# Forgetting attention and RG-LRU trunk on one core: the opening's matmuls in another order, and the forget sum inside the first key tile

## The reference, cut to what matters

```python
proj = x @ w_in
q, k, v, fg = jnp.split(proj, [D_MODEL, 2 * D_MODEL, 3 * D_MODEL], axis=-1)
...
log_f = jax.nn.log_sigmoid((fg + b_f).astype(jnp.float32))
c = jnp.cumsum(log_f, axis=1).transpose(0, 2, 1)
...
logits = jnp.einsum("bhqd,bhkd->bhqk", q_i, k).astype(jnp.float32) * scale
logits = logits + c_i[..., None] - c[:, :, None, :]
...
probs = jax.nn.softmax(logits, axis=-1)
```

## Time and profile before

| | us |
|---|---|
| median of 3 runs | 1261.48 (1260.67 to 1262.12) |
| the profiled execution | 1261.65 |
| its span in the trace | 1259.9 |
| TensorE busy | 1252.0 |
| GpSimd busy | 861.3 |
| VectorE busy | 537.0 |
| ScalarE busy | 408.9 |

### The profile page before, as it was taken

One profiled execution on the slowest core, in us unless ns is written; L12 is line 12 of the kernel. 1 busy time (PEld: TensorE's weight loads), 2 busy tenths in 40 slices (PEclk: granted clock), 3 DMA queues, 4 the chain that ended last, 5 costly groups with the idle time before them and its releaser, 6 DMA issues.

```text
span 1259.9 us, 17776 instructions
## 1 busy us (share of the span) xinstructions
PE 1252.0 (99%) x5893; PEld 1021.6 (81%) x5893; DVE 537.0 (43%) x832; ACT 408.9 (32%) x683; POOL 861.3 (68%) x1155
## 2 busy tenths in 40 slices
PE   9999999999999999999999999999999999999998
PEld 5777778788888888888888778888888888888887
DVE  6545545465344444201343375274444443301352
ACT  4445444224333434100144384014343433200041
POOL 7544557819877877777577646929877788777573
PEclk9999999999999999999999999999999999999999
DMA  5222132303322233333243222312222224333221
GB/s 196 69 67 67 52 115 89 112 17 109 108 88 95 100 122 111 110 92 100 67 167 103 81 84 84 117 51 100 100 100 100 91 93 133 118 100 94 74 92 59
DMA packets 57294, 120.63 MB, mean 96 GB/s; under 512 B 3761, under 2 KB 36081, under 8 KB 56737
## 3 DMA queue, kind: packets, MB, share of 16 engines
q1 hardware_dynamic: 56192, 117.45, 28.3%
q10 hardware_dynamic: 1056, 2.58, 0.6%
HBM read 117.83 MB, written 2.20 MB: 95 GB/s over the span
## 4 chain that ended last, share of the span: by engine, by line
PE 97%; DMA 1%; DVE 1%; ACT 1%; DVEq 0%; issue 0%; ACTq 0%; SPq 0%
PE bank L437 19%; PE bank L439 19%; PE bank L438 19%; PE bank L456 8%; PE bank L457 8%; PE bank L458 8%; PE bank L731 2%; PE bank L738 2%; PE bank L733 2%; PE bank L564 1%; PE bank L551 1%; PE bank L465 1%; PE bank L521 1%; PE bank L523 1%; DMA x<-xT 1%; PE bank L907 1%
## 5 line engine op out<-in xcount | busy, mean ns | idle before, releaser
L423 POOL TENSOR_TENSOR w_lo<-stage,w_hi 128x256 fp32r<-128x256 f32 x800 | 593.7, 773 | 29.5 <-issue 1.5
L417 POOL TENSOR_SCALAR w_hi<-stage 128x1024 fp32r<-128x1024 f32 x200 | 213.4, 1067 | 175.3 <-PE bank L458 77.3
L437 PE MATMUL bank<-x_hi,w_hi 128*128 128x512 f32 (+1 forms) x712 | 275.6, 387 | 0.0
L439 PE MATMUL bank<-x_hi,w_lo 128*128 128x512 f32 (+1 forms) x712 | 275.3, 387 | 0.0
L438 PE MATMUL bank<-x_lo,w_hi 128*128 128x512 f32 (+1 forms) x712 | 275.3, 387 | 0.0
L438 PEld LDWEIGHTS bank<-x_lo,w_hi 128*128 128x128 f32 x712 | 133.7, 188 | 27.3
L437 PEld LDWEIGHTS bank<-x_hi,w_hi 128*128 128x128 f32 x712 | 133.7, 188 | 27.1
L439 PEld LDWEIGHTS bank<-x_hi,w_lo 128*128 128x128 f32 x712 | 133.7, 188 | 26.9
L1150 DVE SCALAR_TENSOR_TENSOR tmp<-bank,cols,tmp 128x511 f32<-128x511 f32 x88 | 66.0, 750 | 201.3 <-ACT tmp L1431 190.3
L415 POOL TENSOR_TENSOR waiter<-waiter 128x1 f32<-128x1 f32 x101 | 21.1, 209 | 171.3 <-PE bank L439 119.0
L456 PE MATMUL bank<-w_hi,h_hi 128*128 128x512 f32 x352 | 137.3, 390 | 0.0
(11 more groups left out here) (182 smaller groups left out, 1806.5 us busy)
## 6 DMA issues: line engine op xcount, KB each, us to landing
stage<-w_square SPq DMA_DIRECT2D x163, 512.0 KB, 3.2
stage<-w_down SPq DMA_DIRECT2D x44, 512.0 KB, 3.6
rows<-norm_rows SPq DMA_DIRECT2D x4, 1024.0 KB, 6.2
outT<-x SPq DMA_DIRECT2D x7, 256.0 KB, 2.0
x<-xT SPq DMA_DIRECT2D x3, 512.0 KB, 6.9
p_in<-pT ACTq DMA_DIRECT2D x2, 512.0 KB, 3.4
w_ai<-w_lru SPq DMA_DIRECT2D x1, 1024.0 KB, 9.4
stage<-w_square ACTq DMA_DIRECT2D x1, 512.0 KB, 7.2
```

The source lines that it names most:

```text
L417: whole = pool.tensor_scalar(high[:, s, :], stage[:, s, :], 1.0, 0.0, ALU.mult, ALU.add)
L423: piece = pool.tensor_tensor(low[:, s, to], stage[:, s, to], high[:, s, to].bitcast(F32), ALU.subtract)
L437: pe.matmul(out, w_hi[:, s, c:c + P], m_hi, start=first, stop=False)
L439: return pe.matmul(out, w_lo[:, s, c:c + P], m_hi, start=False, stop=last)
```

## The change

On TensorE the first two blocks are turned ahead of the first forget products, as soon as the first pair of x is there. The high pass of the first query tile is cut in two: k = 0 to 3 stand behind blocks 2 and 3, and so ahead of the forget products of x tiles 4 to 7; k = 4 to 7 stand behind block 4. `sum_forget` moves from behind the key tile into it, behind step k = 5. On VectorE `c_rows` is made ahead of `queries(0)`. On ScalarE the store of `c_rows` stands ahead of the key tile's copies, and the load of pair 0's rows directly behind them. Since the first blocks may now be turned before the forget products have read their tiles of x, ScalarE's copy back waits for the third block at least.

```diff
--- before.py
+++ after.py
@@ -43,6 +43,7 @@
 QUAD = 32
 PIECES = 4
 WARM_UP = 11
+SUM_AT = 5
 
 TURN_AT = 2
 FIRST_AT = (1, 1, 5)
@@ -607,18 +608,28 @@
             pe.wait_ge(warm_set, 1)
             for n in range(WARM_UP):
                 pe.matmul(banks[7][:], warm[:, 0:P], warm[:], start=True, stop=True)
+            def high_pass(ks):
+
+                pe.wait_ge(first_high, 1)
+                for k in ks:
+                    pe.wait_ge(x_hi_ready, k + 1)
+                    first_pass(w_hi, in_hi, k, first=(k == 0))
+
+            pe.wait_ge(consts_set, 1)
+            pe.wait_ge(x_loaded[0], 16)
+            first_block(0)
+            first_block(1)
             pe.wait_ge(fg_padded, 2)
-            pe.wait_ge(consts_set, 1)
             for n in range(KT // 2):
                 pe.wait_ge(x_loaded[n], 16)
                 forget(2 * n)
                 forget(2 * n + 1)
-                for m in {0: (0, 1), 1: (2, 3), 2: (), 3: (4,)}[n]:
-                    first_block(m)
-            pe.wait_ge(first_high, 1)
-            for k in range(KT):
-                pe.wait_ge(x_hi_ready, k + 1)
-                first_pass(w_hi, in_hi, k, first=(k == 0))
+                if n == 1:
+                    first_block(2)
+                    first_block(3)
+                    high_pass(range(4))
+            first_block(4)
+            high_pass(range(4, KT))
             turn_forget()
             unit_ready(qkv, 0, 0)
             for k in range(KT):
@@ -631,8 +642,7 @@
             mm.then_inc(unit_used, 1)
             first_block(7)
             pe.wait_ge(x_tok_ready, 5)
-            project(0, 1, 1)
-            sum_forget()
+            project(0, 1, 1, {SUM_AT: sum_forget})
             turn_columns()
             project(0, 2, 5)
             pe.wait_ge(x_tok_ready, KT)
@@ -1106,12 +1116,12 @@
                 dve.sem_inc(o_read, 1)
 
             dve.sem_inc(o_read, 1)
-            queries(0, False)
             dve.wait_ge(fg_summed, 1)
             dve.tensor_copy(c_rows[:, 0, :], banks[7][0:HEADS, :])
             dve.drain()
             dve.tensor_tensor(c_rows[:, 1, :], banks[7][0:HEADS, :], c_rows[:, 0, :].bitcast(F32),
                               ALU.subtract).then_inc(fg_rows, 1)
+            queries(0, False)
             keys_low(0)
 
             dve.wait_ge(lam_exp, 1)
@@ -1317,7 +1327,7 @@
 
             def first_block_rows(m):
 
-                act.wait_ge(block_turned, m + 1)
+                act.wait_ge(block_turned, max(m + 1, 3))
                 act.wait_ge(x_lo_ready, m + 1)
                 act.copy(x[:, m, :], banks[BLOCK_BANK[m]][:]).then_inc(x_tok_ready, 1)
 
@@ -1328,6 +1338,11 @@
             for m in range(5, KT):
                 first_block_rows(m)
 
+            def key_rows(j):
+                act.dma_start(k_a[HEAD_DIM:HEAD_DIM + 2, :, :].bitcast(F32),
+                              c_dram.rearrange("(j h) s n -> j s h n", h=2)[bass.ds(j, 1), :, :, :]
+                              .rearrange("a s h n -> (a s) h n")).then_inc(row_loaded, 16)
+
             def key_tiles(j):
                 for to in (k_a, k_b):
                     for h in range(2):
@@ -1335,22 +1350,18 @@
                 act.drain()
                 act.sem_inc(kv_read, 1)
 
+            act.wait_ge(fg_rows, 1)
+            act.dma_start(c_dram, c_rows[:].bitcast(F32)).then_inc(fg_stored, 16)
             act.wait_ge(unit_used, phases["qkv"].done(0, 1))
             key_tiles(0)
+            act.wait_ge(fg_stored, 16)
+            key_rows(0)
             act.wait_ge(flat_done, 1)
             act.copy(flat[:].rearrange("p a n -> p (a n)"), banks[6][0:32, P:P + DEPTH * P]).then_inc(flat_read, 1)
-            act.wait_ge(fg_rows, 1)
-            act.dma_start(c_dram, c_rows[:].bitcast(F32)).then_inc(fg_stored, 16)
             act.wait_ge(lam_abs, 1)
             act.activation(lam4[:, 1, :], lam4[:, 1, :], ACT.Exp, scale=-1.0).then_inc(lam_exp, 1)
-            act.wait_ge(fg_stored, 16)
             act.wait_ge(cols_loaded, 16)
 
-
-            def key_rows(j):
-                act.dma_start(k_a[HEAD_DIM:HEAD_DIM + 2, :, :].bitcast(F32),
-                              c_dram.rearrange("(j h) s n -> j s h n", h=2)[bass.ds(j, 1), :, :, :]
-                              .rearrange("a s h n -> (a s) h n")).then_inc(row_loaded, 16)
 
             def keys(j):
                 act.wait_ge(unit_used, phases["qkv"].done(j, 1))
@@ -1407,7 +1418,6 @@
 
             act.sem_inc(pt_read, 1)
             act.sem_inc(exp_ready, 1)
-            key_rows(0)
             act.wait_ge(flat_read, 1)
             act.dma_start(rows_dram.rearrange("l r n -> r l n"), flat[:]).then_inc(flat_stored, 16)
             values(0, False)
```

## The result

| | before | changed |
|---|---|---|
| median, us | 1262.14 (20 runs) | 1263.98 (20 runs) |
| lowest to highest | 1260.51 to 1263.98 | 1263.47 to 1264.40 |
| the profiled execution | 1261.65 | 1264.34 |
| its span | 1259.9 | 1262.6 |

A forecast was written before the change was run, and what follows sets the result against it. TensorE, busy 99% of the span, was taken as the bound, carrying its position at 44 us to the end. The wait before head 1's scores absorbs -0.1 and -0.6, giving +1.7: 1261.65 to 1263.35, less 0.17, 1263.2 us; range 1261.2 to 1264.6.

The forecast's parts named there:

- products 0.43 us apart behind the idle time: Sign of being wrong: TensorE's matmuls 0.43 us apart after the gap near 42 us, the pace at the lower clock.
- Opening, -0.1: TensorE's opening: turn_forget near 14.28 instead of 14.39, held by z_chan; -0.1 us of the 0.5 the order frees.
- Forget sum, 1.45 earlier, no wait: Forget sum on TensorE starts behind k = 5 at 24.47 instead of 25.92, its input being ready at 23.10.
- Rows landed at 33.9: Load of the key rows, issued by ScalarE at about 31.5 behind the key tile's copies, lands at 33.9.
- queries behind c_rows, first scores at 34.2, released by k_b: VectorE: queries run 28.65 to 32.5, keys ready near 34.1, first scores about 34.2 instead of 34.79, -0.6 us.
- lam operations to 40.6: VectorE's sixteen lam operations, from 34.2, some held by GpSimd, end near 40.6, +2.7 us, ahead of head 0's maxima.
- exp_ready 3.56 behind the maxima: Head 0's exp_ready at 44.15; TensorE waits about 2.3 us, and scores of head 1 start at 44.2, +1.7 us.
- normalise and the maxima of head 1 follow at +1.7 too: Behind the scores of head 1: both steps +1.7 us later, each waiting for TensorE again, so no further loss.
- Rival B: The 2.3 us idle near 42 us lowers TensorE's clock, costing 1.5 to 3 us; total +3.2 to +4.7; chance 0.10.
- The base: The profiled execution of the kernel before, 1261.65 us, to which the sum added 1.7.

The follow-up runs named there:

- the filled gap: Changed kernel with eight products of zeros on TensorE in the wait before the scores of head 1 of the first pair: 1263.55 us, ratio 1.0012 against before.
- the key copies first: Changed kernel with queries(0) ahead of c_rows again and the key tile's copies ahead of the store of c_rows on ScalarE: 1264.13 us, ratio 1.0019 against before.

## Why the prediction was right

It gave 1263.2 us, range 1261.2 to 1264.6, and +1.7 us; measured were 1263.98 and +1.8. The sign, the place and the mechanism up to the scores of head 1 were right; that the number came out so close is in part luck. Between the two profiled executions, on which the sum was built, the change costs 2.7 us and not 1.7: 1.3 at the scores of head 1 (predicted 1.7), and 1.4 behind them, where the sum has nothing. One of the prediction's own signs of being wrong came: products 0.43 us apart behind the idle time. Its parts, in the order of its steps:

- *Opening, -0.1.* Measured 0: turn_forget at 14.40 against 14.38, behind z_chan (13.51 + 0.74). Right in substance.
- *Forget sum, 1.45 earlier, no wait.* Measured 1.35 (24.57).
- *Rows landed at 33.9.* The load was issued at 31.35 (predicted 31.5), and TensorE did not wait for it; when it landed, the trace does not show.
- *queries behind c_rows, first scores at 34.2, released by k_b.* Mis-sized: 33.99, with no wait at all, so -0.8 and not -0.6, and k_b released nothing. The pause of 0.5 us between the two c_rows instructions, which I carried over from before, was gone (26.93 + 0.68, then 27.68), so the keys were ready at 33.60, 0.5 earlier than forecast. The pause is 0.5 us in every kernel that makes c_rows behind queries, and absent in every one that makes it ahead of them; why, no run tells.
- *lam operations to 40.6.* 40.11, maxima at 40.17: 0.5 earlier, as the start was. The way of counting, held ones ending with GpSimd's pieces and free ones at 0.24, held to 0.1 us: five were held, as forecast.
- *exp_ready 3.56 behind the maxima.* 3.56, at 43.73. The stall was 2.1 us on the prediction's way of counting, from the time at which TensorE could have started (41.66; predicted 2.3), of which the trace shows 1.94 as idle; the scores of head 1 started at 43.76, +1.3 in the profiled executions (predicted +1.7).
- *"normalise and the maxima of head 1 follow at +1.7 too."* This step failed. The normalisation took 2.70 instead of 1.28, because it now ran beside GpSimd's split (it came 2.3 us later, and the split 0.9 earlier, from 42.25), so the maxima of head 1 started at 46.90 instead of 44.21, +2.7 and not +1.7. The experiment with the filled gap shows a second wait of 0.61 behind it, and the one with the key copies first one of 0.56. No term of the sum held this.
- *Rival B, the low clock, at 0.10.* It came in about half of the twenty runs, if the slower group is the one with the low clock, as its mean clock, its trace and the filled gap say. It was priced at 1.5 to 3 us on top; it costs 0.7, since it takes the place of the second wait. The forecast and B were not alternatives: the changed kernel shows both. The Trainium skill, in "TensorE: Matmul & The Clock Gate" (why this matters for your kernels), warns that idle gaps of TensorE between bursts of matmuls bring the lower clock back, but of longer gaps than this one. The trace shows a granted clock of 0.5 behind 1.94 us of idle time already, and the full clock with the gap filled.
- *The base.* The sum was set on an execution of before at 1261.65. Before and its variants wait for the rows 0.7, 0.9 or 1.6 us in the traces taken, and its matmuls not at all in one with late maxima. Its profiled execution was a favourable one, 0.5 below its median.

So the total is right partly by compensation: the scores of head 1 started 0.4 earlier than the sum had them, the second wait or the low clock added 0.7 to 1.4 that it did not have, and the base, 0.5 below before's median, took most of that out of the difference of the medians again. What the runs do show as the cause is narrower than "queries behind c_rows": the first way to the late keys is VectorE's order, and close behind it stand two more (the key tile's copies behind the store, and the lam exponential behind the wait for the store); and it is the sixteen lam operations ahead of the first maxima that turn late keys into a wait. Undoing the first way, or the first two, does not help; moving the lam operations does. Late maxima alone, made in the kernel before, give the change's ratio.

## What to carry to other kernels

When an input is made early at the cost of work that stood in its waiting time, follow that work to the end of its engine's list: here 0.8 us gained at one wait became 2 us lost at the next, through small operations that nobody needed soon. Undoing a suspected cause and seeing no change does not clear it while a second way of the same length stands beside it; taking away what all ways lead to does. And put long chains of tiny operations where the neighbour engine that holds them is mostly idle: the same sixteen took 4.5 us there, 6.4 in the opening and 9.5 at the layer norm.

## What the runs showed of the hardware

- An idle time of TensorE of 1.6 to 2.5 us, once the kernel was running, was followed by about 3 us at half clock in every trace that has one: after 1.59 (37 to 40 us), 1.70, 1.90, 1.94 (45.5 to 48.5), 2.38, 2.45 and 2.46 (254 to 256). After 1.46 us in the kernel with the key copies first, and after 0.73 to 0.86 us in others, the clock stayed full. It did not come in every run: by times and mean clock, in ten of twenty of the changed kernel.
- The same store of the running sums landed 1.93 to 2.44 us after its issue, and the load 2.40 to 3.01 us, in one execution each of different kernels; once the load was there sooner, since the scores that need it started at 33.82, 1.6 us after its issue at 32.20. That before's spread of 3.5 us comes from these two transfers and the clock behind them is argued from these traces, not shown.
- Small VectorE operations on SBUF alone (128x8) that ran beside a GpSimd instruction ended with it, after 0.5 to 0.9 us instead of 0.17, in every kernel of this study: in the changed kernel one ended at 35.67, where GpSimd's w_hi ended at 35.64. The normalisation, on SBUF too, took twice its time there (2.70 against 1.28 us).
